# A second sum buffer for the modulation vector, and its third piece started in a later stage

## The reference, cut to what matters

```
mod = (jax.nn.silu(c) @ w_ada[l] + b_ada[l]).reshape(b, N_SUB, 3, D_MODEL)   # 1 x 1024 @ 1024 x 9216

def sublayer(h, i, fn, resid_w):
    shift, scale, gate = mod[:, i, 0, None, :], mod[:, i, 1, None, :], mod[:, i, 2, None, :]
    u = rms_norm(h, norm_pre[l, i]) * (1.0 + scale) + shift
    return h + resid_w * gate * rms_norm(fn(u), norm_post[l, i])

h = sublayer(h, 0, swiglu_2 ..., 0.5); h = sublayer(h, 1, token_mixer ..., 1.0); h = sublayer(h, 2, swiglu_2 ..., 0.5)
```

## Time and profile before

| | us |
|---|---|
| median of 3 runs | 1822.84 (1822.32 to 1831.43) |
| the profiled execution | 1828.06 |
| its span | 1826.4 |
| PE busy in the span | 1713.1 (94%) |
| DVE busy | 992.3 (54%) |
| ACT busy | 821.5 (45%) |
| POOL busy | 581.0 (32%) |
| DMA, share of 16 engines by SP's loads and by POOL's | 47.0% and 6.8% |

### The profile page before, as it was taken

One profiled execution on the slowest core, in us unless ns is written; L12 is line 12 of the kernel. 1 busy time (PEld: TensorE's weight loads), 2 busy tenths in 40 slices (PEclk: granted clock), 3 DMA queues, 4 the chain that ended last, 5 costly groups with the idle time before them and its releaser, 6 DMA issues.

```text
span 1826.4 us, 21892 instructions
## 1 busy us (share of the span) xinstructions
PE 1713.1 (94%) x7939; PEld 1421.0 (78%) x7939; DVE 992.3 (54%) x984; ACT 821.5 (45%) x966; POOL 581.0 (32%) x378
## 2 busy tenths in 40 slices
PE   6999999999999999979879999999997987789998
PEld 5888779878888888768767888788886875678886
DVE  4445668575655565643466645654456433565444
ACT  6565541454445344424344444544445455554343
POOL 0000000188885888852888900000000010500000
PEclk9999999999999999979878999999998997789999
DMA  6656453267784778645334765546563521425552
GB/s 215 204 186 212 147 192 110 91 218 243 243 263 147 255 238 260 228 157 189 93 117 159 231 197 185 178 147 193 186 214 119 208 92 47 138 92 185 186 185 88
DMA packets 208278, 321.35 MB, mean 176 GB/s; under 512 B 10920, under 2 KB 146402, under 8 KB 208226
## 3 DMA queue, kind: packets, MB, share of 16 engines
q1 hardware_dynamic: 195968, 281.05, 47.0%
q0 software_dynamic: 10512, 38.54, 6.8%
q10 hardware_dynamic: 1746, 1.05, 0.2%
HBM read 319.55 MB, written 1.05 MB: 176 GB/s over the span
## 4 chain that ended last, share of the span: by engine, by line
PE 74%; POOL 9%; DVE 7%; ACT 5%; issue 4%; DMA 1%; ACTq 0%; POOLq 0%; SPq 0%; DVEq 0%
PE ps L544 21%; PE ps L546 21%; PE ps L545 21%; POOL arena L508 3%; POOL arena L505 3%; DVE w_lo L1606 2%; POOL arena L510 2%; PE ps L590 1%; PE ps L842 1%; ACT w_hi L1181 1%; PE ps L780 1%; PE ps L648 1%; POOL arena L512 1%; PE ps L597 1%; PE ps L947 1%
## 5 line engine op out<-in xcount | busy, mean ns | idle before, releaser
L1606 DVE TENSOR_TENSOR w_lo<-raw,w_hi 128x2048 fp32r<-128x2048 f32 x256 | 630.7, 2472 | 326.1 <-ACT w_hi L1181 325.9
L544 PE MATMUL ps<-w_hi,actT_hi 128*128 128x512 f32 x1504 | 605.6, 403 | 21.1 <-DVE actT_lo L1634 7.8
L546 PE MATMUL ps<-w_hi,actT_lo 128*128 128x512 f32 x1504 | 594.5, 395 | 0.0
L545 PE MATMUL ps<-w_lo,actT_hi 128*128 128x512 f32 x1504 | 594.4, 395 | 0.0
L1181 ACT CAST w_hi<-raw 128x2048 fp32r<-128x2048 f32 x266 | 506.1, 1911 | 192.1 <-PE ps L546 190.4
L544 PEld LDWEIGHTS ps<-w_hi,actT_hi 128*128 128x128 f32 x1504 | 288.3, 192 | 82.5 <-DVE actT_lo L1634 8.5
L546 PEld LDWEIGHTS ps<-w_hi,actT_lo 128*128 128x128 f32 x1504 | 287.5, 191 | 62.5
L545 PEld LDWEIGHTS ps<-w_lo,actT_hi 128*128 128x128 f32 x1504 | 288.5, 192 | 57.7
L544 PE MATMUL ps<-w_hi,hT_hi 128*128 128x512 f32 x480 | 188.1, 392 | 2.6 <-DVE hT_lo L1731 2.6
L545 PE MATMUL ps<-w_lo,hT_hi 128*128 128x512 f32 x480 | 187.5, 391 | 0.0
L546 PE MATMUL ps<-w_hi,hT_lo 128*128 128x512 f32 x480 | 187.5, 391 | 0.0
(11 more groups left out here) (255 smaller groups left out, 1455.4 us busy)
## 6 DMA issues: line engine op xcount, KB each, us to landing
raw<-ffn_w_in_dram SPq DMA_DIRECT2D x176, 512.0 KB, 4.8
raw<-ffn_w_out_dram SPq DMA_DIRECT2D x88, 512.0 KB, 4.4
arena<-w_ada_dram POOLq DMA_DIRECT2D x72, 512.0 KB, 5.0
raw<-ffn_w_gate_dram SPq DMA_DIRECT2D x44, 512.0 KB, 3.9
raw<-ffn_w_up_dram SPq DMA_DIRECT2D x44, 512.0 KB, 4.9
raw<-ffn_w_down_dram SPq DMA_DIRECT2D x44, 512.0 KB, 4.5
raw<-w_in_dram SPq DMA_DIRECT2D x40, 512.0 KB, 4.5
raw<-hg_w_in_dram SPq DMA_DIRECT2D x32, 512.0 KB, 4.6
```

What stands on the lines that cost most here:

```text
L544: nc.tensor.matmul(to, hi, whi, start=start, stop=False, skip_group_check=True)
L545: nc.tensor.matmul(to, hi, wlo, start=False, stop=False, skip_group_check=True)
L546: return nc.tensor.matmul(to, lo, whi, start=False, stop=stop, skip_group_check=True)
L1606: nc.vector.tensor_tensor(w_lo[:, s, :], raw[:, s, :], w_hi[:, s, :].bitcast(F32), ALU.subtract)\
```

## The change

`ada_acc` becomes a list of regions: pieces 0 and 2 stay at column 12288, piece 1 gets its own at 8192 (3072 columns). POOL therefore starts piece 1 right after piece 0, with no wait for `ada_reduced`. After piece 1 it makes the gate weights of `fox_in`, and only then waits for `ada_reduced` 2 and for `turned`, the transposes of both tiles of `fox_out`, before it starts piece 2. PE gets a wait for the constants' load ahead of the first `ada_reduce`.

```
-        ada_acc = region(12288, ADA_W)
+        ada_acc = [region(at, ADA_W) for at in (12288, 8192, 12288)]
...
-            for piece in range(3):
-                if piece:
-
-                    pool.wait_ge(ada_reduced, piece)
+            def ada_piece(piece):
                 for s in range(2):
                     ada_load(piece, s, s)
-                if piece == 2:
-                    split_gate_weights(by_name["fox_in"])
                 with pool.Fori(0, ADA_N // 2 - 1) as i:
...
+            ada_piece(0)
+            ada_piece(1)
+            split_gate_weights(by_name["fox_in"])
+            pool.wait_ge(ada_reduced, 2)
+            pool.wait_ge(turned, 4 * (by_name["fox_out"].turned + 1))
+            ada_piece(2)
             pool.wait_ge(ada_reduced, 3)
...
             def ada_reduce(piece):
+                if piece == 0:
+                    pe.wait_ge(consts_loaded, 16)
                 pe.wait_ge(ada_summed, ADA_N * (piece + 1))
```

More of the change, by code:

```diff
@@ L511, in ada_unit @@
                 pool.wait_ge(ada_by2, n + 1)
-                nc.gpsimd.tensor_tensor(ada_acc[:, bass.ds(u * ADA_U, ADA_U)], r[:, 0, :], r[:, 1, :], ALU.add)\
+                nc.gpsimd.tensor_tensor(ada_acc[piece][:, bass.ds(u * ADA_U, ADA_U)], r[:, 0, :], r[:, 1, :], ALU.add)\
                     .then_inc(ada_summed, 1)
                 pool.wait_ge(ada_summed, n + 1)
-            for piece in range(3):
-                if piece:
-                    pool.wait_ge(ada_reduced, piece)
+            def ada_piece(piece):
                 for s in range(2):
                     ada_load(piece, s, s)
-                if piece == 2:
-                    split_gate_weights(by_name["fox_in"])
                 with pool.Fori(0, ADA_N // 2 - 1) as i:
@@ L779, in ada_reduce @@
                 for u in range(ADA_N):
-                    last = nc.tensor.matmul(ps[:, SMALL_BANK, u:u + 1], ada_acc[:, u * P:(u + 1) * P],
+                    last = nc.tensor.matmul(ps[:, SMALL_BANK, u:u + 1], ada_acc[piece][:, u * P:(u + 1) * P],
                                             C["ones"][:, 0:1], start=True, stop=True)
```

## The result

The changed kernel takes 1815.53 us (median of 12 runs, 1812.36 to 1818.75). The kernel before, timed again beside it, takes 1827.91 (12 runs, 1819.02 to 1831.77). The ratio is 0.994 with a 95% interval of 0.9923 to 0.9957, so the gain is 11 us, between 8 and 14. I had forecast 17.4 us less, a ratio of 0.9905, which lies outside the interval, and a time of 1805.5 us with a range of 1799 to 1813: the measured 1815.53 lies 2.5 us above that range. The direction held; the size did not. The ratio doesn't depend on that base, and it too was missed.

A forecast was written before the change was run, and what follows sets the result against it. PE, busy 94% of the span, bounds the kernel, so only its waits could pay. 14.2 + 4.2 - 1.0 = 17.4 us off 1828.06 gave ratio 0.9905, 1805.5 us from the 1822.84 median, range 1799 to 1813.

The forecast's parts named there:

- that base: Median of the first three runs of the kernel before, 1822.84 us, on which the forecast 1805.5 was built.
- The wait and its 48 matmuls: At piece 1's reduction in `fox_in`: PE's 10.65 us wait goes and its matmuls run at a higher clock; 14.2 us.
- some 3 us: At piece 1's reduction: POOL ends at 789, PE comes at 792.35, so PE no longer waits.
- The attention: Fox attention without POOL: DVE lines 1934 and 1958 shorten, so PE waits less; 4.2 us, ends 0 and 8.4.
- The transitions: Fourth to fifth feed-forward stage: POOL's last units now lie there and cost 1 us, ends 0 and about 4.
- The one behind `fox_out`: Transition from `fox_out`: no cost counted, since POOL works there before and after the change.
- The rule that I had quoted against the change: Shared SBUF ports: VectorE operations with two SBUF inputs and GpSimd block each other for whole instructions, also in the new transition.
- The third piece in time: Fourth feed-forward stage: piece 2 ends at 1189.3 in old time, before ACT's gate row at 1195.55; cost zero.
- The third rival: Piece 2 ends too late, ACT's gate row and PE wait, kernel slower, up to 1880 us; chance 0.03.
- The first: Attention gives nothing as ACT or score matmuls end last; collisions move to the new transition; 10.2 us less, chance 0.13.
- The second: Piece 1 still ends late, at 795, PE waits 3 us and the clock falls; 10.9 us less, chance 0.06.
- The sum: Whole kernel: 14.2 + 4.2 - 1.0 = 17.4 us less, ratio 0.9905.

The follow-up runs named there:

- the run with the pause: The change with the third piece cut in two, 4 units in `fox_in`, 20 from the fourth feed-forward stage on; 1809.9 us, 0.9911 of the kernel before.
- the buffer alone: The kernel before with only the second sum buffer, third piece still beside the attention; 1818.3 and 1817.8 us, ratio 0.9943.
- the buffer with fill: The kernel before with the second sum buffer and 38 extra matmuls in PE's attention waits, third piece not moved; 1810.2 us, ratio 0.9894.

## Why the prediction was wrong, step by step

**The wait and its 48 matmuls: 14.2 us.** Mechanism right, size 1 us too high. From the start of the transition into `fox_in` to the attention the kernel before takes 120.1, 119.3 and 119.3 us, the changed one 106.9 and 106.0: 13.1 less by the means. The margin of "some 3 us" was 1.3 us in one trace of the change and negative in the other (PE waited 2.28), at a cost of 4 us, in the trace whose transition was 5 us shorter. The 48 matmuls took 7.96 and 9.51 us in the two, not the 6.03 of the third piece's, so that their part of the term was 2.4 and 0.9 us. I counted the units' pace from one stretch and took the quick end for the last ones, just where DVE and POOL collide most: the last unit took 10.4 us.

**The attention: 4.2 us.** As a statement on what VectorE's freed steps are worth it was near: line 1934 came down to 4.49 us (I had 4.58) and line 1958 to 0.17, and GpSimd's absence is worth 3.4 us at equal clock, and 2.9 over the stages that the clock moves. As a statement on the stage it failed. The sum took the stage as fixed but for the two waits, and "the lower end is 0" had an engine that ends last as its worst case; the first traces have +2.3 us instead (attention and `fox_out`, 110.0 to 112.3), below that bound, and the means of three and two traces 112.0 and 112.3, no gain. What the step lacked was a term for PE's clock: three traces of the same kernel lie 5.8 us apart there, at 0.79 and 0.72. For the time of the whole kernel this matters less than for the stage, since the token mixer moves the other way. The row that I needed stood on the page of before, part 2, the granted clock in 40 slices:

```profile
PEclk9999999999999999979878999999998997789999
```

Most of the attention is in the twentieth and twenty-first slice, at 0.8 and 0.7, in a row of nines. I priced the clock of the 48 matmuls and left out that of this stage, and took one trace's draw for the kernel's.

**The transitions: 1 us. This is the term that was most mis-sized for the kernel's time:** by the means of three and two traces they cost 4.3 us, 3.3 more than I had put, and the run with the pause gets them back. The one into the fifth feed-forward stage costs 2.2 to 2.6 us in every trace with POOL busy in it for 13 us (41.3, 41.7, 41.5, 40.9, against 38.9 to 39.3 in eight with at most 3 us of POOL in it, and 40.5 and 40.4 in two more at a lower clock); my ends were 0 and 4, and the value I took came from the transition where the collision had happened to hurt least. The one behind `fox_out` I put at nothing, since POOL works in it before and after. That reason did not hold: it is 19.1 in all three traces of before and 20.7 to 21.2 in the changed ones, with 17 us of POOL's work in it before and 18 to 19 after; what collides seems to depend on where POOL's units fall, which is argued and not shown. One trace of the buffer alone has 21.2 too, so this cost is not tied to the change.

In the transition into the fifth stage the cost can be seen on PE and DVE, after:

```profile
1175.72 1.20 PE L598 MATMUL ps<-w_hi,actT_lo 128*128 128x512 f32 x4 [1.55 <-DVE actT_lo L1637]
...
1183.63 1.19 PE L598 MATMUL ps<-w_hi,actT_lo 128*128 128x512 f32 x4 [0.72 <-DVE actT_lo L1637]
```

```profile
1168.64 3.38 DVE L1609 TENSOR_TENSOR w_lo<-raw,w_hi 128x2048 fp32r<-128x2048 f32 x1
...
1174.52 1.15 DVE L1637 TENSOR_TENSOR actT_lo<-arena,actT_hi 128x512 fp32r<-128x512 f32 x1
...
1175.78 1.59 DVE L1643 TENSOR_SCALAR arena<-x,small 128x1024 f32<-128x1024 f32 x1
```

The split took 3.38 us, not 2.29; the second activation part 1.15, where the next of its kind took 0.69, behind POOL's end; PE waited 2.27 us for it in two, a wait that before does not have. By the Trainium skill ("SBUF — State Buffer", Who interferes with whom) a VectorE operation with two SBUF inputs, or a tensor_scalar in a two-port mode, and a GpSimd operation shut each other out, and the one that issued first keeps the shared ports for its whole instruction. These three fit that: when the split started, POOL's running addition had 1.2 us to go, and the split took 1.1 longer; POOL's next addition (line 510 there) took 2.67 us, where the one of the unit before took 0.74, and ended 0.6 us after the split. The rule that I had quoted against the change was the one to weigh higher.

**The third piece in time.** Right. POOL starts it at 963.50 and ends it at 1178.51, 7 to 8 us behind my numbers; ACT's gate row came at 1189.38, 11 us later, so that neither it nor PE's reduction was held up. The third rival did not occur.

**The rivals.** The first gave 10.2 us less, near the measured 11, and by its sign (the attention as long as before) it holds. It was right that the collisions move into the transitions, at its full 4 us. Its reason for the attention, that ACT or the score matmuls end last there, is not what the traces show: at equal clock the stage is 3.4 us shorter. So its number came out in part by luck. The second gave 10.9: its late piece was seen in one of two traces, but its sum still held 4.2 us from the attention and 1 us of transitions, so its number is luck too.

**The sum.** Between the first traces the stall gives 13.2 us less, attention and `fox_out` 2.3 more, the transitions 4.2 more and the token mixer 4.9 less: 11.6 less, where the spans differ by 10.1; the remaining 1.5 lie in small pieces over the other stages. By the means of all traces of the two kernels it is 13.1 for the stall, 2.9 for attention, `fox_out` and token mixer together, less 4.3 for the transitions: 11.7 us, against 11.0 by the ratio and 12.4 by the medians. Of the 5.7 us that this lacks to my 17.4, 3.3 are the transitions, 1.3 the attention and 1.1 the stall. The step that failed for the time is thus the price of POOL's work in the transitions, and for the attention's length the missing clock.

What stays open: why the clock falls in one execution and not in another from the same instructions, and why a short attention comes with a long token mixer. Whether the two groups of runs of the buffer with fill are the same thing isn't shown, since only one of them was traced.

## What to carry to other kernels

Where a stage alternates short matmuls with waits of 1 to 4 us, its clock is a term of the sum: take the spread of the stage over several traces before pricing a wait in it, and check whether another stage moves the other way before blaming the total on it. Try filling the waits: here it gave some 12 us on top of the 16 of the reordering, and 8 on the kernel before, but nothing in the token mixer. Background work on GpSimd is best put under a stage that is bound by matmuls and stopped before the transitions: each that it touches can cost 2 us, and whether it does is hard to tell beforehand, as the same work cost nothing behind `fox_out` before the change. A buffer that lets a late engine start 17 us earlier buys the lateness seen, here 10.65 us, and little more, and a margin of 3 us is none where the clock moves the other engine by 5.

## What the runs showed of the hardware

Filling PE's waits with 38 matmuls of 512 columns raised the granted clock of the attention from 0.76 to 0.91 and shortened it by 11 us (one trace each), although the matmuls were added to the busiest engine. By the Trainium skill ("TensorE: Matmul & The Clock Gate", Loop structure matters more than you think) long waits for DMA between matmuls let the clock drop. This stage shows the same with waits of 1.2 to 3.3 us that end on VectorE or ScalarE.

The clock can also fall where PE has no gap. Before the 48 one-column matmuls of the changed kernel PE was busy for 11.15 us on end at 1.00; in their 7.96 us, all busy, it was 0.66, and 0.65 in the 6.79 us behind, all busy too. In the kernel before, the third piece shows 1.00 for 10.97 us ahead, then 0.86 and 0.64.

In the nine traces without fill a short attention stands beside a long token mixer: in the same kernel 86.8 us at 0.79 and 95.8 at 0.82 in one execution, 92.6 at 0.72 and 91.0 at 0.86 in another.
